# In the routing of a mixture of experts, TensorE's transposes of the next tile stand in front of the router's products of this one

## The chip, the cores and the metric

The program runs on one core of one Trainium2 chip. The metric is the device time of one execution in microseconds (us). TensorE multiplies and transposes, VectorE and ScalarE work on its results in the accumulation banks, GpSimd issues the gathers and scatters of rows, and SyncE issues the loads of the weights. Each engine runs its own instructions in the order in which they are written; between engines there are semaphores only.

## The reference, cut to what matters

Two blocks follow one another on 1024 tokens of width 1024. The second block has two layers, and each of them ends in the same mixture of experts, in which the experts choose their tokens:

```python
def expert_choice_moe(x, w_router, w_gate_up, w_down):
    B, S, _ = x.shape
    cap = CAPACITY_FACTOR * S // N_EXPERTS          # 128 tokens an expert
    aff = jax.nn.softmax((x @ w_router).astype(jnp.float32), axis=-1)
    gates, idx = lax.top_k(jnp.swapaxes(aff, 1, 2), cap)
    xs = x[bi, idx]
    g, u = jnp.split(jnp.einsum('becd,edf->becf', xs, w_gate_up), 2, axis=-1)
    out = jnp.einsum('becf,efd->becd', jax.nn.silu(g) * u, w_down) * gates[..., None]
    return jnp.zeros_like(x).at[bi, idx].add(out)
```

The change touches only how `x @ w_router` and its softmax are ordered on TensorE. There are 16 experts.

## The kernel before, in words

`moe` (from line 4210) is called once a layer, so twice. Its routing goes over the 1024 tokens in NT = 8 tiles of 128, in a loop `for k in range(NT + 2)` that stands once for each engine. Three sets of buffers are used in turn, `u = k % 3`: the banks 2u and 2u+1 belong to a set. For one tile the work is this chain:

1. T, TensorE, L4417: eight transposes of the tile of X into banks 2u and 2u+1. From tile 3 on, the first of them waits until VectorE has taken the affinities of the tile three back out of the same bank (`aff_taken`).
2. Copies, ScalarE, L4613: two copies, four blocks each, out of the two banks (even, odd) into a row of work memory that the trace names first_block or m_spare.
3. Products, TensorE, L4410: 16 small products with the router's weights, in two halves. The first waits for the even copy, the second for the odd one. Four strips of 32 partitions of bank 2u each collect a part of the sum.
4. Raw copy, ScalarE, L4627: the bank into m_logits.
5. Fold, TensorE, L4424: two products that add the four strips and turn the result round; it waits for the raw copy (`taken`).
6. Softmax: maximum and its negative on VectorE (L4797, L4799), exponential on ScalarE (L4618), reciprocal and scaling on VectorE (L4801, L4803).
7. One iteration of the loop later: the spread (L4386) and the turned affinities (L4433) on TensorE, the row copy on ScalarE (L4623), the copy of the turned affinities on VectorE (L4807, which frees the bank for T), and on VectorE a number of counts (L4751) for the rank of every token with expert 0. The number of counts grows with the tile.

The orders are written out by hand. In iteration k TensorE does: products of tile k-1, T of tile k, fold of tile k-1, spread and turned affinities of tile k-2. ScalarE does: the two copies of tile k, the exponential of tile k-1, the row copy of tile k-2, and last the raw copy of tile k (which needs the products that TensorE has in its iteration k+1). VectorE does: maximum to scaling of tile k-1, then copy and counts of tile k-2. From k = 8 on there is no T, and TensorE runs filler products of no use (`keep`, L180) that keep it busy.

When the loop is over, VectorE finishes the counts, ranks the tokens (L4774) and marks the chosen ones (L4780), TensorE multiplies them out to a list (`list_tensor`, L4392), runs 48 filler products, and waits for the list and for the rows that GpSimd gathers by it (L5025). These are transposed (L4447) and copied (L4643), and the products of expert 0 begin (L4461). SyncE has loaded the weights of expert 0 since the start of the stage.

The functions in question are given here with their lines.

Of the kernel before, what the change touches and what calls it, by code (L numbers as in the profile page):

```python
# [13 lines left out]
P = 128  # L14

D = 1024
KD = D // P
# [6 lines left out]
NT = SEQ // P  # L24
# [4185 lines left out]
def moe(k, c, ps, io, layer, X, rows, out, sb):  # L4210
# [7 lines left out]
    with stage(k, sb) as st:  # L4218
# [18 lines left out]
        turned, even, odd, logits, maxed, exped, inverted, affed, aff_turned, aff_taken = (st.sem(n) for n in (  # L4237
            "turned", "even_copied", "odd_copied", "logits", "maxed", "exped", "inverted", "affed", "aff_turned", "aff_taken"))
# [146 lines left out]
        def spread_tensor(pe, x, t):  # L4385
            pe.transpose(spread_bank(x, t), aff[:, t, x:x + 1].broadcast_to([P, P]), c["ident"][:, :]).then_inc(*spread[x].up())  # L4386
# [8 lines left out]
        def tensor(pe):  # L4395
            def keep(n):
                keep_streaming(pe, core, ps[5], n)

            pe.matmul(ps[7][:, 0:P], c["ones"][:, :], c["before"][:, :]).then_inc(*placed.up())
            for k in range(NT + 2):  # L4400
                if 1 <= k <= NT:
                    u = (k - 1) % 3
                    if k == 1:
                        pe.wait_ge(*router_in)
                    pe.wait_ge(even.sem, k)
                    for d in range(KD):
                        if d == 4:
                            pe.wait_ge(odd.sem, k)
                        q = slice(QUARTER * (d % 4), QUARTER * (d % 4) + QUARTER)
                        m = pe.matmul(ps[2 * u][q, 0:P], wr[:, d, :], spare[u][:, d, :], start=d < 4, stop=d >= 4)  # L4410
                    m.then_inc(*logits.up())
                if k < NT:
                    u = k % 3
                    if k >= 3:
                        pe.wait_ge(aff_taken.sem, k - 2)
                    for b in range(KD):
                        m = pe.transpose(ps[2 * u + b // 4][:, (b % 4) * P:(b % 4) * P + P], X[:, k, b * P:(b + 1) * P],  # L4417
                                         c["ident"][:, :])
                        if b % 4 == 3:
                            m.then_inc(*turned.up())  # L4420
                if 1 <= k <= NT:
                    u = (k - 1) % 3
                    pe.wait_ge(taken.sem, k)
                    pe.matmul(ps[2 * u + 1][:, 0:NE], raw[u][:, :], c["fold"][:, :]).then_inc(*brought.up())  # L4424
                if k >= 2:
                    u = (k - 2) % 3
                    pe.wait_ge(affed.sem, k - 1)
                    if k == 2:
                        pe.wait_ge(places_in.sem, 1)
                    elif k >= 4:  # L4430
                        pe.wait_ge(row_in.sem, k - 3)
                    spread_tensor(pe, 0, k - 2)
                    pe.transpose(ps[2 * u][0:NE, 0:P], aff[:, k - 2, 0:NE], c["ident"][:, :]).then_inc(*aff_turned.up())  # L4433
                if k >= NT:
                    keep(8)
# [647 lines left out]
        g, b = (spare[i][:, :, :].rearrange("p k t -> p (k t)") for i in range(2))  # L5083
# [20 lines left out]
        nc.gpsimd.memset(eps[:, :], LN_EPS).then_inc(*eps_set.up())  # L5104
        sync(nc.sync)
        tensor(nc.tensor)
        scalar(nc.scalar)
        vector(nc.vector)
# [96 lines left out]
```

## Time and profile before

| | |
|---|---|
| median of three runs | 3791.79 us (3790.16 to 3795.48) |
| the profiled execution's own time | 3789.95 us |
| its span | 3788.2 us |
| mean granted clock of TensorE | 0.994 |
| TensorE busy | 3679.2 us, 97% |
| VectorE busy | 2225.6 us, 59% |
| ScalarE busy | 1109.6 us, 29% |
| DMA, mean over the span | 152 GB/s |

The span runs from the first to the last instruction. A busy TensorE is not one at its peak: the filler counts as busy, and matmuls overlap. The routing of the first of the two layers lies at 1920 to 1966 us of the span, that of the second at 3069 to 3113 us.

### The profile page before, as it was taken

Reading aid. Unit: us, or ns where it says so; the run is one execution under the profiler, and the core shown is the slowest. Engines: PE = TensorE matmul, PEld = TensorE weight load, DVE = VectorE, ACT = ScalarE, POOL = GpSimd, SP = SyncE. Lnnn points to the kernel's source line nnn. Section 1 sums busy time; section 2 is a strip of 40 time slices with the busy share of each in tenths; the row PEclk is TensorE's granted clock in tenths of the full one; section 3 lists DMA queues with packets and bytes.
Section 4 is the critical chain, followed back from the end, with each engine's and each line's share of the span. In section 5 each row is a group of like instructions: output and inputs, shape, how many; then the busy total and the mean of one; then the engine's idle time right before and its main releaser. Section 6 shows DMA issues by size and latency. Waiting matters only on the chain. (4 is left out here: it accounts for less than half of the span.)

```text
span 3788.2 us, 63983 instructions
## 1 busy us (share of the span) xinstructions
PE 3679.2 (97%) x26734; PEld 1976.0 (52%) x26734; DVE 2225.6 (59%) x3869; ACT 1109.6 (29%) x2363; POOL 572.3 (15%) x709
## 2 busy tenths in 40 slices
PE   8999999999999999999999999998999999999998
PEld 5565756767586745545554433434444454343333
DVE  2234334666666645356667656664577788665664
ACT  2343313344353401046630111113343431111113
POOL 3332002011010022100001111110132201111110
PEclk9999999999999999999999999999999999999999
DMA  5101111000101052210069999996211259999996
GB/s 115 29 29 42 29 29 47 18 13 20 29 4 46 5 184 62 45 34 18 17 236 338 349 333 345 348 327 243 63 45 38 96 212 347 341 348 335 346 337 226
DMA packets 267326, 574.31 MB, mean 152 GB/s; under 512 B 49264, under 2 KB 123920, under 8 KB 267040
## 3 DMA queue, kind: packets, MB, share of 16 engines
q1 hardware_dynamic: 251776, 520.93, 38.9%
q0 software_dynamic: 9504, 34.61, 4.0%
q10 hardware_dynamic: 5760, 14.68, 1.0%
q8 instruction: 213, 3.49, 0.4%
q14 instruction: 73, 0.60, 0.0%
HBM read 521.93 MB, written 48.23 MB: 151 GB/s over the span
## 5 line engine op out<-in xcount | busy, mean ns | idle before, releaser
L4461 PE MATMUL bank<-ring,m_hidden_T 128*128 128x512 f32 x1024 | 449.4, 595 | 1.5 <-ACT m_hidden_T L4661 1.5
L4461 PEld LDWEIGHTS bank<-ring,m_hidden_T 128*128 128x128 f32 x1024 | 191.3, 190 | 232.6 <-issue 228.2
L4475 PE MATMUL bank<-ring,m_chosen 128*64 128x512 f32 x832 | 192.1, 604 | 4.0 <-POOL m_chosen L5041 4.0
L4475 PE MATMUL bank<-X,m_chosen 128*64 128x512 f32 x832 | 187.3, 592 | 0.0
L4881 DVE TENSOR_TENSOR m_junk<-bank,m_junk 128x512 f32<-128x512 f32 x26 | 18.0, 692 | 267.8 <-PE bank L4475 267.8
L4461 PE MATMUL bank<-ring,m_picked_T 128*128 128x512 f32 x384 | 167.9, 593 | 4.4 <-ACT m_picked_T L4643 2.4
L1683 PE MATMUL bank<-hnT,first_block 128*128 128x320 f32 (+3 forms) x512 | 167.7, 478 | 0.7 <-PEq L104 0.7
L4656 ACT ACTIVATE m_hidden<-m_junk 128x512 f32<-128x512 f32 x26 | 16.4, 632 | 447.6 <-DVE m_junk L4895 447.6
L4475 PEld LDWEIGHTS bank<-ring,m_chosen 128*64 128x64 f32 x832 | 58.2, 138 | 130.3 <-issue 124.6
L1683 PEld LDWEIGHTS bank<-hnT,first_block 128*128 128x128 f32 x512 | 94.5, 190 | 54.4 <-issue 11.7
L4858 DVE TENSOR_TENSOR X<-ring 128x1024 f32<-128x1024 f32 x104 | 122.5, 1221 | 0.0
L4868 DVE TENSOR_TENSOR X<-X,ring 128x1024 f32<-128x1024 f32 x104 | 122.2, 1217 | 0.0
L4475 PEld LDWEIGHTS bank<-X,m_chosen 128*64 128x64 f32 x832 | 59.8, 137 | 118.9 <-issue 118.9
L3401 PE MATMUL bank<-a_weights,xT 128*128 128x512 f32 x256 | 119.3, 594 | 1.3 <-DMA a_weights<-in_attn_w_o 1.3
L4461 PEld LDWEIGHTS bank<-ring,m_picked_T 128*128 128x128 f32 x384 | 72.0, 190 | 92.6 <-issue 89.8
L5070 POOL DMA_INDIRECT y_rows<-m_ys,m_tokens x30 | 47.7, 1590 | 480.4 <-issue 394.7
L1859 PE MATMUL bank<-rw_lane 64*64 64x64 f32 x2720 | 111.7, 224 | 8.7 <-issue 2.2
L532 PE MATMUL bank<-hnT,w_block 128*128 128x512 f32 (+3 forms) x304 | 119.4, 534 | 0.0
L4713 ACT ACTIVATE m_ys<-bank,m_gates 128x512 f32<-128x512 f32 x30 | 20.6, 687 | 328.9 <-PE bank L4461 328.9
L5025 POOL DMA_INDIRECT m_picked<-mix,m_tokens x32 | 53.5, 1673 | 408.1 <-PE bank L4447 217.8
L532 PE MATMUL bank<-hnT,first_block 128*128 128x512 f32 (+3 forms) x320 | 112.0, 501 | 0.6 <-PEq L104 0.6
L1859 PEld LDWEIGHTS bank<-rw_lane 64*64 64x64 f32 x2720 | 95.9, 133 | 28.9 <-issue 22.0
(683 smaller groups left out, 7691.9 us busy)
## 6 DMA issues: line engine op xcount, KB each, us to landing
ring<-in_moe_w_gate_up SPq DMA_DIRECT2D x90, 2048.0 KB, 9.6
ring<-in_moe_w_down SPq DMA_DIRECT2D x256, 512.0 KB, 4.9
ring<-in_moe_w_gate_up SPq DMA_DIRECT2D x96, 512.0 KB, 9.6
m_second_ring<-in_moe_w_gate_up SPq DMA_DIRECT2D x14, 2048.0 KB, 13.6
first_block<-in_w_in SPq DMA_DIRECT2D x23, 512.0 KB, 3.9
w_block<-in_w_in SPq DMA_DIRECT2D x19, 512.0 KB, 4.2
mix<-X SPq DMA_DIRECT2D x16, 512.0 KB, 2.6
ring<-y_rows SPq DMA_DIRECT2D x16, 512.0 KB, 8.4
```

The source lines that it names most:

```text
L532: x = pe.matmul(bank_of(s + j)[:, 0:w], wb[b % RING][:, d, :], hnT[:, d, col:col + w], start=d == 0, stop=d == KD - 1)
L1683: m = pe.matmul(banks[j][:, 0:n], wb[i % 3][:, d, :], hnT[:, d, col:col + n], start=d == 0, stop=d == KD - 1)
L1859: x = pe.matmul(L.tall(0)[side(d), h, i, :], power_t(L, e, d, h, i), power(L, e, d, h, i))
L3401: x = pe.matmul(ps[6 + half][:, :], oT[:, b, t * P:(t + 1) * P], weights[:, b, 512 * half:512 * half + 512], start=b == 0, stop=b == KD - 1)
L4461: m = pe.matmul(banks[j][:, :], lhsT[:, (i % 8) * P:(i % 8 + 1) * P], ring[:, i, j, :], start=i % 8 == 0, stop=i % 8 == KD - 1)
L4475: m = pe.matmul(bank[tok[half], :], tokens_(j), weights(j)[:, 512 * half:512 * half + 512], start=j == 0, stop=j == 3)
L4713: ac.activation(ys[:, 0:512], ps[6][:, :], ACT.Copy, scale=gates[:, e:e + 1]).then_inc(*y_even.up())
L4858: ve.tensor_tensor(t2(j), quarter(e, 2, j), quarter(e, 1, j), ALU.subtract).then_inc(*w_summed.up())
L4868: ve.tensor_tensor(t2(j), t2(j), quarter(e, 3, j), ALU.subtract).then_inc(*w_summed.up())
L4881: ve.tensor_tensor(u2[:, :], ps[1][:, :], first_kept[:, :], ALU.add).then_inc(*joined.up())
L5025: gp.indirect_dma_start(xg[:, :], None, rows_saved[:, :], bass.IndirectOffsetOnAxis(ap=tokens[:, e:e + 1], axis=0)).then_inc(*gathered.up(16))
L5070: gp.indirect_dma_start(y_rows[:, :], bass.IndirectOffsetOnAxis(ap=tokens[:, e:e + 1], axis=0), ys[:, :], None, compute_op=ALU.add).then_i ...
```

## The change

In TensorE's program the eight transposes of tile k are put in front of the products of tile k-1. Iteration k is now: T of tile k, products of tile k-1, fold of tile k-1, spread and turned affinities of tile k-2. The waits move along with their instructions. No instruction is added or taken away, and nothing is changed in the programs of the other engines.

```diff
             for k in range(NT + 2):
+                if k < NT:
+                    u = k % 3
+                    if k >= 3:
+                        pe.wait_ge(aff_taken.sem, k - 2)
+                    for b in range(KD):
+                        m = pe.transpose(ps[2 * u + b // 4][:, (b % 4) * P:(b % 4) * P + P], X[:, k, b * P:(b + 1) * P],
+                                         c["ident"][:, :])
+                        if b % 4 == 3:
+                            m.then_inc(*turned.up())
                 if 1 <= k <= NT:
                     u = (k - 1) % 3
                     if k == 1:
                         pe.wait_ge(*router_in)
                     pe.wait_ge(even.sem, k)
                     ...
                     m.then_inc(*logits.up())
-                if k < NT:
-                    u = k % 3
-                    if k >= 3:
-                        pe.wait_ge(aff_taken.sem, k - 2)
-                    for b in range(KD):
-                        m = pe.transpose(ps[2 * u + b // 4][:, (b % 4) * P:(b % 4) * P + P], X[:, k, b * P:(b + 1) * P],
-                                         c["ident"][:, :])
-                        if b % 4 == 3:
-                            m.then_inc(*turned.up())
                 if 1 <= k <= NT:
                     u = (k - 1) % 3
                     pe.wait_ge(taken.sem, k)
                     pe.matmul(ps[2 * u + 1][:, 0:NE], raw[u][:, :], c["fold"][:, :]).then_inc(*brought.up())
```

## Rows read from the trace of the kernel before

**Rows 1.** Chain that ended last, second layer: start us, us, what.
```profile
3079.85 1.09 ACT first_block L4613 x2
3084.66 1.90 DVE m_junk L4751 x12
3104.29 6.74 PE bank L180 x48
3111.03 0.89 PE bank L4447 x8
```

**Rows 2.** Timeline, TensorE, second layer: start, us, engine, line, operation [idle before].
```profile
3071.51 1.09 PE L4417 MATMUL bank<-ident,X 128*128 128x128 f32 x8
...
3076.43 1.09 PE L4417 MATMUL bank<-ident,X 128*128 128x128 f32 x8 [0.48 <-DVE m_aff L4807]
3077.36 0.29 PE L4424 MATMUL bank<-fold,m_logits 128*128 128x16 f32 x2
...
3077.84 0.84 PE L4410 MATMUL bank<-first_block,router 128*32 128x128 f32 x16
3079.16 1.09 PE L4417 MATMUL bank<-ident,X 128*128 128x128 f32 x8 [0.48 <-DVE m_aff L4807]
...
3087.94 1.09 PE L4417 MATMUL bank<-ident,X 128*128 128x128 f32 x8 [0.96 <-DVE m_aff L4807]
...
3090.59 0.40 PE L4424 MATMUL bank<-fold,m_logits 128*128 128x16 f32 x2 [0.40 <-ACT m_logits L4627]
```

**Rows 3.** Timeline, TensorE's weight loads for the second half of one tile's products, second layer.
```profile
3078.26 0.16 PEld L4410 LDWEIGHTS bank<-first_block,router 128*32 128x32 f32 x8 [0.26 <-ACT first_block L4613]
```

**Rows 4.** Timeline, VectorE, second layer.
```profile
3077.68 0.17 DVE L4797 TENSOR_REDUCE m_st<-bank 128x1 f32<-128x16 f32 x1 [0.77 <-PE bank L4424]
3077.89 0.15 DVE L4799 TENSOR_SCALAR m_st<-m_st 128x1 f32<-128x1 f32 x1
3078.49 0.16 DVE L4801 RECIPROCAL m_st<-m_st 128x1 f32<-128x1 f32 x1 [0.45 <-ACT m_aff_tiles L4618]
3078.69 0.23 DVE L4803 TENSOR_SCALAR m_aff_tiles<-m_aff_tiles,m_st 128x16 f32<-128x16 f32 x1
3078.83 0.27 DVE L4807 COPY m_aff<-bank 16x128 f32<-16x128 f32 x1
...
3090.35 0.27 DVE L4807 COPY m_aff<-bank 16x128 f32<-16x128 f32 x1
```

**Rows 5.** Timeline, ScalarE, second layer.
```profile
3077.12 1.09 ACT L4613 ACTIVATE first_block<-bank 128x512 f32<-128x512 f32 x2 [0.82 <-PE bank L4417]
3078.09 0.28 ACT L4618 ACTIVATE m_aff_tiles<-bank,m_st 128x16 f32<-128x16 f32 x1
...
3078.75 0.28 ACT L4627 ACTIVATE m_logits<-bank 128x128 f32<-128x128 f32 x1
...
3090.26 0.28 ACT L4627 ACTIVATE m_logits<-bank 128x128 f32<-128x128 f32 x1
```

**Rows 6.** DMA issues, 3104 to 3113 us: KB each (none for indirect ones), median us to landing.
```profile
m_picked<-mix,m_tokens POOLq DMA_INDIRECT x1, 4.4
```

**Rows 7.** Windows of 1 us, TensorE, first layer: length, busy (instructions), granted clock, DMA share, GB/s.
```profile
1923.00:1924.00 1.00, 1.00 (x14) 0.50 1.23 215
```

**Rows 8.** Windows, second layer: length, then busy (instructions) of TensorE, its loads, VectorE, ScalarE, GpSimd; clock.
```profile
3104.00:3106.00 2.00, 2.00 (x11) 2.00 (x11) 1.67 (x9) 0.00 (x0) 0.65 (x1) 0.50 0.19 76
```

**Rows 9.** Timeline, TensorE, first layer.
```profile
1923.52 1.97 PE L4417 MATMUL bank<-ident,X 128*128 128x128 f32 x8
1929.28 1.09 PE L4417 MATMUL bank<-ident,X 128*128 128x128 f32 x8 [0.48 <-DVE m_aff L4807]
1940.78 1.09 PE L4417 MATMUL bank<-ident,X 128*128 128x128 f32 x8 [0.96 <-DVE m_aff L4807]
```

**Rows 10.** Timeline, TensorE and GpSimd, around the list of expert 0, second layer.
```profile
3101.99 2.30 PE L4392 MATMUL bank<-m_aff_tiles,m_chosen 128*128 128x17 f32 x16 [1.21 <-DVE m_chosen L4780]
3105.35 0.98 POOL L5025 DMA_INDIRECT m_picked<-mix,m_tokens  x1 [35.98 <-DVE m_gates L4785]
```

## The prediction

> **What bounds the kernel now.** I read the page's first two parts, then the chain of waits, then the timeline of the routing engine by engine. The chain runs almost wholly over TensorE's expert products, but in both layers it also runs through the routing, end to end: VectorE's counts, ScalarE's copies, the filler, the transposes of the gathered rows [rows 1]. So a microsecond in the routing is a microsecond of the kernel, unless something near its end gives it back. Time was lost in the routing although no engine is full: T of tile 3 starts at 3076.43, T of tile 4 at 3079.16, and ahead of each TensorE sits idle 0.48 us for VectorE's copy [rows 2]. The routing is a ring of waits over three engines.
>
> The ring before, tile 3 to tile 4, start to start: T to fold 0.93 (3076.43 to 3077.36) [rows 2]; fold to maximum 0.32, to the negative 0.21 [rows 4]; to the exponential 0.20 (3078.09) [rows 5]; to the reciprocal 0.40, to the scaling 0.20, to the copy 0.14 [rows 4]; to the next T 0.33 (3079.16) [rows 2]. Sum 2.73 us. The products are not in this ring: they run at 3077.84 to 3078.68, behind the fold and ahead of the next T, while VectorE and ScalarE work on the softmax, and the raw copy (3078.75) [rows 5] is done long before the next fold asks for it. They look slow, 0.84 us with a wait of 0.26 us for the odd copy in the middle [rows 2, 3], but it lies beside the softmax and costs nothing.
>
> **The change part by part.** Nothing is added; two pieces change places on TensorE. T of tile k+1 still can't start before VectorE's copy. Behind it now come the products of tile k, whose operands were copied a tile ago, and only then the fold of tile k, which needs the raw copy of those products. What lay beside the softmax is put into the ring.
>
> *The ring after.* T to the first product 0.93, as T to fold before. The products no longer wait. How long do sixteen take in one go? Eight take 0.42 from first start to last end (3078.26 to 3078.68), with weights loaded in 0.16 [rows 2, 3]; sixteen take 0.42 + 0.16 = 0.58 if the second eight follow at the pace of the loads. Below: all within 0.42. Above: 0.84, as with the waits. I take 0.58, since the loads' pace is the nearest row. Last end to raw copy 0.07 (3078.68 to 3078.75) [rows 2, 5]. So the raw copy starts at 0.93 + 0.58 + 0.07 = 1.58 after T. Raw copy to fold 0.33 (3090.26 to 3090.59, the one case where TensorE waited for it) [rows 5, 2]: 1.91. To the exponential by VectorE 0.32 + 0.21 + 0.20: 2.64. But there is a second rule: ScalarE does the raw copy of tile k before the two copies of tile k+1, and before the exponential. In front of it the copies start 0.69 after T (3077.12) and the exponential stands 0.97 behind their start [rows 5]. Now they start only behind the raw copy, at 1.58 + 0.16 (its 0.28 less the overlap of some 0.12 that the two copies show, 1.09 us for a pair of which the second ends 0.12 after the next start) = 1.74, and the exponential can start at 2.71. This is later than 2.64, so it decides. Then 0.40 + 0.20 + 0.14 + 0.33 as before: 3.78 us. The ring grows by 1.05.
>
> The Trainium skill, "TensorE: Matmul & The Clock Gate", section "Part 3: Packing small matmuls — row/col tiling", has it that products that write different strips of 32 partitions run at once, three of them 2.38 times as fast as one by one. The rows agree with it as far as they go, since the loads of eight products are through in 0.16 us and the last ends 0.26 us later. By that rule the sixteen would lie nearer the lower bound, 0.42, and the ring would be 3.62.
>
> *VectorE's counts* stood in the ring for the late tiles: T of tile 7 waits 0.96 [rows 2]. From copy to the next possible maximum there are now 0.33 + 1.91 + 0.32 = 2.56 us, of which the counts can use 2.36 (they start 0.20 behind the copy), and for tile 3 they last 1.90 [rows 1], so they go under: T of tile 3 to T of tile 7 took 11.51 (3076.43 to 3087.94; first layer 1929.28 to 1940.78, 11.50) [rows 2, 9] and will take 4 x 3.78 = 15.12. That is +3.61 a layer. Behind T of tile 7 the order on TensorE is the old one, and VectorE full of counts is the bound. Its copy came 2.41 after T (3090.35) [rows 4] and now comes at 2.71 + 0.74 = 3.45: +1.04. All counts, the list and the gather shift with it.
>
> *The first tiles* gain. T of tile 1 starts right behind T of tile 0, at 3070.32 in place of 3071.51 [rows 2]. By the same steps the raw copy of tile 0 comes at 3071.9 and T of tile 2 at 3072.4; products of tile 1 start behind it (3073.33) and T of tile 3 at 3076.2: -0.2. In the first layer the clock is at half there (0.50 in 1923 to 1924, T of tile 1 1.97 us long) [rows 7, 9]; T and the products now both stand ahead of the first fold in this stretch, and the gain is eaten: 0.
>
> Sum so far: first layer 3.61 + 1.04 = 4.65, second 4.45; together +9.1.
>
> *The end of the routing.* GpSimd issues the gather at 3105.35 and it has landed 4.4 later, 3109.75 [rows 6, 10], but the transposes of its rows start only at about 3110.9, behind the filler [rows 1]. Of a delay there up to 1.1 us a layer could come back, if the filler runs at full clock (a part of it ran at half [rows 8]). Where the low stretch falls after a shift of over 4 us I can't tell: -0.1 on the whole, with ends 0 and -2.2. Weights of expert 0 have landed before the list in both cases, so they hide nothing; the expert stage behind starts as it did, only later.
>
> Forecast: +9.0. On the profiled execution, 3789.95, that is 3799.0. The median of the runs shown is 1.84 higher, 3791.79, so the median after should be 3800.8.
>
> **The rivals.**
>
> (a) *The clock falls inside the ring.* TensorE now works about 2.1 us of 3.78 a tile, with an idle stretch of some 1.3 us where 0.48 stood. Against a fall: idle 0.96 before T of tile 7 did not bring it down. For: in both layers it fell after the idle 1.21 before the list [rows 10, 8] (and in the first before 1923 [rows 7]). At the lower of its levels (1.2 GHz in place of 2.4) T lasts 1.97 in place of 1.09 [rows 9], +0.88, and the products and the fold lose another 0.4. At 1.3 us a tile and two to five such tiles a layer this is +5 to +13 on top, about 3808. The skill's same page, "A second HAM failure mode: psum-queue depth-cycling", tells of small pauses between groups of matmuls that make the clock go down and up; no row of this ring shows it so far.
>
> (b) *Muted.* Products at 0.42 (-0.16 in each of 5 rings and twice in the first tiles, -1.1 a layer) and the filler's slack used in full (-1.1 a layer): 9.1 - 4.4 = 4.7, time 3796.5. For it speaks that strips overlap, against it that both must be at their end.
>
> (c) *Faster.* T ahead of the products starts the two copies earlier, and the products find their operands ready. If the copy to T wait were not what holds T, the 1.2 us by which T of tile 1 is early would be kept in each layer, and the idle 0.48 ahead of T would go in five tiles a layer: -2.4 to -7.2, 3784.6 to 3789.4. It decides if fold does not have to wait for the raw copy. The rows speak against it: the idle ahead of T names the VectorE copy, which stands behind the fold, and the raw copy can't precede its products.
>
> **How the numbers follow.** Forecast 0.52 (its own range 3799.0 to 3804.5: products between the pace of the loads and 0.84, +0.26 in 12 rings at most), (a) 0.25, (b) 0.19, (c) 0.04. The range goes from 3796 to 3811. What can be told from no change is about 0.2%, 7.6 us, which is 3799.4. Forecast and (a) lie above it but for a small part of the forecast's case: slower 0.76, same 0.20, faster 0.04.
>
> **What would show it.** Start to start of T in tiles 3 to 7 at 3.78, not 2.73; idle ahead of T for VectorE's copy grown to 1.3 or so; a new idle stretch of TensorE of 0.4 ahead of every fold, released by the raw copy; the copies (L4613) directly behind the raw copy; no wait left ahead of the products. TensorE's granted clock below 1 between T of tile 3 and T of tile 7 would be (a). If T follows T by under 3.4 us, or the list comes less than 3.5 us later behind the stage's start, the sum is wrong; if T follows T by 2.73 or less, the reasoning is.

## The result: 14 us slower, a ratio of 1.0042

The changed kernel takes 3805.05 us (median of six runs, 3803.64 to 3811.04) against 3790.97 us (six runs, 3786.28 to 3795.48): ratio 1.0042, 95% interval 1.0032 to 1.0051. The profiled execution took 3805.19 us with a span of 3803.4 us; before 3789.95 and 3788.2. The forecast was slower by 9.0 us, 3800.8, with a range of 3796 to 3811. Direction, mechanism and range held; the slowdown was 5 us more than forecast.

T of tile 0 of the first layer stands at 1924.39 in place of 1921.13, with the same instructions ahead of it. Two kernels with nearly the time of before have it at 1924.5 and 1924.6 (first_tiles and b_bank2, below; b_bank2 has the old order), so these 3.3 us aren't tied to the change. Everything below is measured from T of tile 0 in each layer.

The counts of TensorE's matmuls in all texts here are those of the trace. It lists each f32 product of the program as two instructions and each transpose as one: the fold is one `pe.matmul` and stands as x2, the products of a tile are eight and stand as x16, `keep(24)` stands as x48.

The routing after, TensorE, second layer, one tile and the end of the ring (start, us, engine, line, operation [idle before]); T is now L4406, the products L4419:

```profile
3093.09 1.09 PE L4406 MATMUL bank<-ident,X 128*128 128x128 f32 x8 [1.24 <-DVE m_aff L4807]
3094.11 0.64 PE L4419 MATMUL bank<-first_block,router 128*32 128x128 f32 x16
3095.16 0.40 PE L4424 MATMUL bank<-fold,m_logits 128*128 128x16 f32 x2 [0.40 <-ACT m_logits L4627]
...
3097.05 1.09 PE L4406 MATMUL bank<-ident,X 128*128 128x128 f32 x8 [1.24 <-DVE m_aff L4807]
...
3101.01 1.09 PE L4406 MATMUL bank<-ident,X 128*128 128x128 f32 x8 [1.24 <-DVE m_aff L4807]
3102.04 1.08 PE L4419 MATMUL bank<-first_block,router 128*32 128x128 f32 x16
3103.52 0.61 PE L4424 MATMUL bank<-fold,m_logits 128*128 128x16 f32 x2 [0.40 <-ACT m_logits L4627]
...
3106.95 3.62 PE L180 MATMUL bank<-ones 128*128 128x128 f32 x16
```

Before, T followed T at 2.73 us with 0.48 idle ahead of it [rows 2]. Now it is 3.96 us, 1.24 idle ahead of T, and 0.40 idle ahead of the fold, released by the raw copy (m_logits). The products have no wait any more. Behind T of tile 7, at 3101.01, the same products take 1.08 in place of 0.64 us and sixteen filler matmuls 3.62 us: the clock has fallen, as the windows below show. ScalarE's timeline in the same tile:

```profile
3094.82 0.28 ACT L4627 ACTIVATE m_logits<-bank 128x128 f32<-128x128 f32 x1 [2.27 <-PE bank L4419]
3095.00 1.08 ACT L4613 ACTIVATE m_spare<-bank 128x512 f32<-128x512 f32 x2
3095.99 0.27 ACT L4618 ACTIVATE m_aff_tiles<-bank,m_st 128x16 f32<-128x16 f32 x1
```

VectorE's timeline in the same tile:

```profile
3095.59 0.17 DVE L4797 TENSOR_REDUCE m_st<-bank 128x1 f32<-128x16 f32 x1 [1.05 <-PE bank L4424]
3095.80 0.15 DVE L4799 TENSOR_SCALAR m_st<-m_st 128x1 f32<-128x1 f32 x1
3096.38 0.16 DVE L4801 RECIPROCAL m_st<-m_st 128x1 f32<-128x1 f32 x1 [0.43 <-ACT m_aff_tiles L4618]
...
3096.72 0.27 DVE L4807 COPY m_aff<-bank 16x128 f32<-16x128 f32 x1
```

The copies come directly behind the raw copy, as foretold, where they stood 0.69 behind T [rows 5]. The chain of waits of the changed kernel (start, us, what), same layer, behind the ring:

```profile
3117.91 1.71 PE bank L4392 x16
...
3119.87 14.57 DVE m_junk L4751 x72
...
3151.93 0.70 DVE m_hidden L4919
3152.67 0.66 PE bank L4454 x4
```

Here the chain leaves the list (L4392) over VectorE: the 36 counts for expert 1 (72 instructions, a count and the reading of its sum), its ranking, the first rounds of the selection for the other experts, and only then the hidden values of expert 0. In the kernel before it went over the filler, the gathered rows and expert 0 [rows 1]. The two ways are nearly equally long: the transposes of those hidden values (L4454) start 34.9 to 35.0 us behind the list after, and 35.3 to 35.4 before. This matters below.

The windows of TensorE in the changed kernel, second layer (length, busy, instructions, granted clock, DMA share, GB/s):

```profile
3099.00:3102.00 3.00, 1.64 (x12) 1.00 1.04 384
3102.00:3105.00 3.00, 2.60 (x31) 0.51 1.04 410
...
3108.00:3111.00 3.00, 3.00 (x16) 0.50 1.03 410
```

The times in the routing, from T of tile 0 of each layer, in us ("3 to 7" is T of tile 3 to T of tile 7; each from TensorE's timeline):

| kernel | T of tile 3 | 3 to 7 | list | first product of expert 0 |
|---|---|---|---|---|
| before, layer 1 | 8.15 | 11.50 | 33.71 | 44.84 |
| before, layer 2 | 7.05 | 11.51 | 32.61 | 43.75 |
| after, layer 1 | 7.07 | 15.84 | 39.65 | 49.52 |
| after, layer 2 | 7.06 | 15.84 | 39.64 | 49.35 |

The list comes 5.94 and 7.03 us later, together 12.97. Of these, 8.67 come from tile 3 to 7, 5.37 from behind T of tile 7, and 1.07 are gained ahead of tile 3.

### The profile page after: what moved, and what is told of

It is laid out like the page before. It is cut to its first block and busy times, and to the rows that moved or that the text cites. A ratio compares the mean times of both kernels' runs of the same rounds, so it can differ in the third digit from the quotient of the medians.

```text
span 3803.4 us, 63983 instructions
## 1 busy us (share of the span) xinstructions
PE 3684.1 (97%) x26734; PEld 1980.8 (52%) x26734; DVE 2226.9 (59%) x3869; ACT 1107.4 (29%) x2363; POOL 570.2 (15%) x709
## 5 line engine op out<-in xcount | busy, mean ns | idle before, releaser
L4475 PE MATMUL bank<-ring,m_chosen 128*64 128x512 f32 x832 | 192.1, 604 | 4.0 <-POOL m_chosen L5041 4.0
L4475 PE MATMUL bank<-X,m_chosen 128*64 128x512 f32 x832 | 187.3, 592 | 0.0
L4475 PEld LDWEIGHTS bank<-ring,m_chosen 128*64 128x64 f32 x832 | 58.2, 138 | 130.5 <-issue 124.7
L4475 PEld LDWEIGHTS bank<-X,m_chosen 128*64 128x64 f32 x832 | 59.7, 137 | 118.8 <-issue 118.8
```

The lines of the kernel that those rows point to most:

```text
L4475: m = pe.matmul(bank[tok[half], :], tokens_(j), weights(j)[:, 512 * half:512 * half + 512], start=j == 0, stop=j == 3)
```

## The experiments

Medians in this section are those of the runs of one chip, each with the ratio to the kernel before on that chip (3790.08, 3789.84 and 3790.05 us in the three sets). List times are from T of tile 0, first and second layer.

**The changed kernel once more** (a_again, no edit).

> The changed kernel once more. Theory: the change costs what the routing shows, so the ring (T of tile 3 to T of tile 7) is 15.8 us in both layers against 11.5, T of tile 0 to the first product of expert 0 about 49.4 us, and the total 10 to 13 us over the kernel before. T of tile 0 of the first layer, which stood 3.3 us later in the changed kernel's trace, isn't tied to the change: it can stand anywhere from 1919 to 1926. Rival: the 3.3 us ahead of the routing belong to the change as well and stand there again (1924 or later), total 14 us or more.

3809.26 us, ratio 1.0054 (1.0040 to 1.0067). In its trace tile 3 to 7 is 16.69 and 15.84, first product at 50.29 and 49.39, T of tile 0 at 1924.00. The trace agrees with the theory within a few tenths but for one tile. The median, 19 us over the kernel before, is above the 10 to 13 expected. In the first layer something was left out of the theory:

```profile
1942.95 1.28 PE L4406 MATMUL bank<-ident,X 128*128 128x128 f32 x8 [1.24 <-DVE m_aff L4807]
1944.16 1.08 PE L4419 MATMUL bank<-m_spare,router 128*32 128x128 f32 x16
...
1947.76 1.97 PE L4406 MATMUL bank<-ident,X 128*128 128x128 f32 x8 [1.00 <-DVE m_aff L4807]
```

T to T is 4.81 us here: the clock fell inside the ring (0.50 from 1946 to 1949 us). This costs 0.85 us, and the profiled execution took 3804.21 us, the fastest of the five, so this trace alone doesn't show where the 19 us come from. The runs' mean granted clocks point at more such falls: of the eleven runs of this kernel five have 0.993 or 0.994 and 3803.6 to 3805.2 us; the six with 0.990 to 0.992 have 3808.1 to 3814.4 us. None of the six was traced. T of tile 0 stands at 1924.00, just at the rival's mark, but the rival, that the 3.3 us ahead of the routing belong to the change, falls with b_bank2, which has the old order and 1924.56.

**The idle ahead of T filled** (a_keep2, against the changed kernel).

```diff
                     pe.transpose(ps[2 * u][0:NE, 0:P], aff[:, k - 2, 0:NE], c["ident"][:, :]).then_inc(*aff_turned.up())
+                if 2 <= k < NT - 1:
+                    keep_streaming(pe, core, ps[2 * ((k - 2) % 3) + 1], 4)
```

> The changed kernel with eight filler matmuls in the idle stretch of 1.24 us ahead of T in tiles 3 to 7. Theory: the ring is waits, not TensorE's work, so it stays 15.8 us from T of tile 3 to T of tile 7 although TensorE does 0.94 us more a tile; the granted clock stays at 1.00 behind T of tile 7, and T of tile 7 to the list falls from 16.7 to about 15.3 us. Total 1 to 3 us under the changed kernel. Rival, TensorE's own work bounds the ring: it grows by up to 0.9 us a tile. Rival, the low clock behind T of tile 7 costs nothing: T of tile 7 to the list stays 16.7.

3799.21 us, ratio 1.0025 (1.0015 to 1.0035), with runs of 3798.0 to 3803.0. Tile 3 to 7 stays 15.85 and 15.84, and T of tile 7 to the list is 15.30 in place of 16.74 in both layers, with the clock at 1.00 in both. TensorE's timeline in one tile of the second layer:

```profile
3090.54 0.64 PE L4419 MATMUL bank<-first_block,router 128*32 128x128 f32 x16
3091.58 0.40 PE L4424 MATMUL bank<-fold,m_logits 128*128 128x16 f32 x2 [0.40 <-ACT m_logits L4629]
...
3092.07 1.06 PE L180 MATMUL bank<-ones 128*128 128x128 f32 x8
3093.48 1.09 PE L4406 MATMUL bank<-ident,X 128*128 128x128 f32 x8 [0.35 <-DVE m_aff L4809]
```

And TensorE's windows behind T of tile 7 of the first layer, columns as above:

```profile
1949.00:1952.00 3.00, 2.60 (x33) 1.00 1.02 407
1952.00:1955.00 3.00, 2.45 (x22) 1.00 1.02 406
```

More work on TensorE made the kernel faster. The ring is not TensorE's work, and the low clock is part of what the change costs. The gain against the changed kernel is 6 to 10 us by the medians, over the 1 to 3 expected. The list accounts for 2.9 of it; the rest would be falls inside the ring in runs that weren't traced, which the expectation left out, but that is not shown. What is left over the kernel before, 9.1 us, is the ring at full clock; the list is later by 4.50 and 5.60 us there, 10.1.

**The move for tiles 0 to 2 alone** (first_tiles, here against the kernel before).

```diff
+                if k < 3:
+                    ...
                 if 1 <= k <= NT:
                     ...
-                if k < NT:
+                if 3 <= k < NT:
```

> The move done for tiles 0 to 2 alone, from tile 3 on the old order. Theory: the loss is in the tiles whose T waits for VectorE's copy. T of tile 3 to T of tile 7 is 11.5 us as before, T of tile 0 to T of tile 3 about 7.1 (before 8.15 and 7.05), total within 2 us of the kernel before. Rival, a T ahead of the products costs something in every tile: T of tile 0 to T of tile 3 grows by about 1 us a tile.

3790.88 us, ratio 1.0002 (0.9993 to 1.0011). T of tile 3 at 7.06 and 7.07, tile 3 to 7 11.51 and 11.50, list 32.63 in both layers. As the theory has it: all the loss is in the tiles whose T waits for VectorE's copy.

**ScalarE's order turned round** (a_scalar_order): the raw copy of tile k-1 behind the copies of tile k, in the changed kernel.

```diff
                     for half, done in enumerate((even, odd)):
                         ...
+                if 1 <= k <= NT:
+                    ac.wait_ge(logits.sem, k)
+                    ac.activation(raw[(k - 1) % 3][:, :], ps[2 * ((k - 1) % 3)][:, 0:P], ACT.Copy).then_inc(*taken.up())
                 ...
-                if k < NT:
-                    u = k % 3
-                    ac.wait_ge(logits.sem, k + 1)
-                    ac.activation(raw[u][:, :], ps[2 * u][:, 0:P], ACT.Copy).then_inc(*taken.up())
```

> The changed kernel, but on ScalarE the raw copy of a tile stands behind the two copies of the next one, no longer ahead of them. Theory (two rules for the exponential, ScalarE's queue deciding by 0.1 us): the copies start 0.7 us behind T, the raw copy stays at 1.73, the exponential comes at 2.79 by VectorE in place of 2.89, and the ring is 3.86 us in place of 3.96. Rival (ScalarE's order alone makes the loss): the ring falls to 3 us or less.

One run, 3805.77 us. The ring is 3.96 us at full clock (second layer), not 3.86: a miss. The raw copy comes at 1.73 and the exponential at 2.89, as without the edit, but now VectorE releases it. TensorE's timeline:

```profile
3090.32 1.09 PE L4406 MATMUL bank<-ident,X 128*128 128x128 f32 x8 [1.24 <-DVE m_aff L4806]
3091.34 0.64 PE L4419 MATMUL bank<-first_block,router 128*32 128x128 f32 x16
3092.38 0.40 PE L4424 MATMUL bank<-fold,m_logits 128*128 128x16 f32 x2 [0.40 <-ACT m_logits L4617]
```

ScalarE's:

```profile
3092.05 0.28 ACT L4617 ACTIVATE m_logits<-bank 128x128 f32<-128x128 f32 x1
3093.21 0.27 ACT L4621 ACTIVATE m_aff_tiles<-bank,m_st 128x16 f32<-128x16 f32 x1 [0.88 <-DVE m_st L4798]
```

VectorE's:

```profile
3092.81 0.17 DVE L4796 TENSOR_REDUCE m_st<-bank 128x1 f32<-128x16 f32 x1 [1.46 <-PE bank L4424]
```

From the fold to the maximum it is 0.43 us, not 0.32: a fold that had to wait takes 0.40, one that follows directly 0.29. By VectorE the exponential is thus also due at 2.89. The two rules meet within a hundredth, and ScalarE's order costs nothing in the ring. Ahead of it T of tile 3 came at 7.29 in place of 7.06 in both layers. And the clock fell inside the ring in both: tile 3 to 7 is 19.79 us in the first layer and 16.59 in the second. The first layer:

```profile
1935.57 1.97 PE L4406 MATMUL bank<-ident,X 128*128 128x128 f32 x8 [0.99 <-DVE m_aff L4806]
...
1940.85 1.09 PE L4406 MATMUL bank<-ident,X 128*128 128x128 f32 x8 [1.25 <-DVE m_aff L4806]
...
1945.38 1.97 PE L4406 MATMUL bank<-ident,X 128*128 128x128 f32 x8 [0.99 <-DVE m_aff L4806]
```

With that, three of the six layers traced with the new order and no filler in it (after, a_again, this one) have a fall inside the ring.

**A bank of its own for the turned affinities** (b_bank2 with the old order, a_bank2 with the new one). T then waits for the exponential of the tile three back.

```diff
                     if k >= 3:
-                        pe.wait_ge(aff_taken.sem, k - 2)
+                        pe.wait_ge(exped.sem, k - 2)
                     ...
+                    if k >= 3:
+                        pe.wait_ge(aff_taken.sem, k - 2)
-                    pe.transpose(ps[2 * u][0:NE, 0:P], aff[:, k - 2, 0:NE], c["ident"][:, :]).then_inc(*aff_turned.up())
+                    pe.transpose(ps[7][0:NE, 0:P], aff[:, k - 2, 0:NE], c["ident"][:, :]).then_inc(*aff_turned.up())
```

VectorE's copy reads bank 7 accordingly. The spread is kept in bank 6 alone and waits for the row copy of the tile before.

> The kernel before, with the turned affinities in a bank of their own (bank 7; the spread then has bank 6 alone), so that T waits for the exponential of the tile three back and no longer for VectorE's copy. Theory: the ring over VectorE's copy is open. T follows T at 2.0 to 2.5 us in tiles 3 and 4 and then runs ahead of VectorE, whose own work (1.35 us plus the counts, 2.4 to 3.2 us a tile) is left as the bound. T of tile 0 to the list falls by 1 to 2 us a layer. Rival (T's place in the order is what counts): no change.

> The changed kernel with the same bank of its own for the turned affinities. Theory: the change costs only because T waits for VectorE's copy and the products and the raw copy then stand behind T in that ring; with the ring open it costs nothing. T of tile 0 to the list within 1.5 us of the kernel before with the same bank, total within 3 us of it, so 10 us or more under the changed kernel. Rival, the fold waits for the raw copy in any case: T of tile 0 to the list stays 3 us or more above the kernel before with that bank.

Old order 3787.74 us, ratio 0.9991 (0.9982 to 1.0000); new order 3788.45 us, 0.9994 (0.9985 to 1.0003). T follows T at 2.19 us with the old order and 2.50 with the new; the list stands at 31.55 and 31.56 against 31.97 and 31.97. TensorE's timeline with the new order, second layer:

```profile
3077.14 1.04 PE L4406 MATMUL bank<-ident,X 128*128 128x128 f32 x8
3078.11 0.64 PE L4419 MATMUL bank<-first_block,router 128*32 128x128 f32 x16
3079.15 0.40 PE L4424 MATMUL bank<-fold,m_logits 128*128 128x16 f32 x2 [0.40 <-ACT m_logits L4629]
...
3079.64 1.04 PE L4406 MATMUL bank<-ident,X 128*128 128x128 f32 x8
```

The 0.40 us ahead of the fold are still there, the 1.24 ahead of T are gone. The move by itself costs 0.4 us a layer up to the list, and the two times can't be told apart; all the rest of its price needs the wait for VectorE's copy.

**The products done twice** (b_twice, a_twice): the loop over d stands over `[*range(KD), *range(KD)]`.

> The kernel before with each tile's sixteen router products done twice over. Theory: the products lie beside the softmax and outside the ring, with 0.48 us of idle behind them, so 0.3 us more a tile cost nothing up to tile 7: T of tile 3 to T of tile 7 stays 11.5 us. Rival (TensorE's work is the bound): it grows by 0.3 us a tile.

> The changed kernel with each tile's sixteen router products done twice over. Theory: here the products are in the ring, so each tile grows by what the second sixteen add, 0.3 to 0.4 us: T of tile 3 to T of tile 7 goes from 15.84 to 17.0 to 17.5 us, the total up by 4 to 6 us. Rival (products outside of the ring here too): stays 15.8.

Old order 3791.56 us, ratio 1.0004 (0.9994 to 1.0013), tile 3 to 7 11.50 and 11.50: nothing in the ring. Ahead of it they do cost: T of tile 3 is at 7.93 in place of 7.05, and the list at 33.50 in place of 32.61 (second layer). TensorE's timeline in the second layer:

```profile
3079.15 1.28 PE L4410 MATMUL bank<-first_block,router 128*32 128x128 f32 x32
3080.47 1.09 PE L4417 MATMUL bank<-ident,X 128*128 128x128 f32 x8
...
3083.21 1.09 PE L4417 MATMUL bank<-ident,X 128*128 128x128 f32 x8
```

T still follows T at 2.74 us: the products fill the idle time that stood ahead of it.

New order 3816.77 us, ratio 1.0069 (1.0054 to 1.0085). At full clock its ring is 4.40 us (first layer, tile 3 to 4), +0.44, what the second sixteen take (1.08 less 0.64). Tile 3 to 7 came out at 22.9 and 21.1 us, over the 17.5 expected, and the total 8 to 12 us over the changed kernel, not 4 to 6, since the clock falls again and again. The windows of TensorE in the second layer:

```profile
3091.00:3095.00 4.00, 2.64 (x45) 1.00 1.03 387
...
3099.00:3103.00 4.00, 3.01 (x23) 0.50 1.05 376
3103.00:3107.00 4.00, 2.36 (x38) 0.93 1.05 391
3107.00:3111.00 4.00, 3.35 (x40) 0.60 1.06 390
```

The same instructions are free inside the old ring and paid in the new one, 0.44 us a tile at full clock: this shows most directly what came into the ring.

**Eight more filler matmuls ahead of the list** (b_keep: kernel before; b_bank_keep: with the bank of its own, old order): `keep(16)` becomes `keep(20)` ahead of `list_tensor(pe, 0, ps[4])`.

> The kernel before with eight more filler matmuls in the idle stretch of 1.2 us ahead of the list of expert 0. Theory: that stretch makes the clock fall, and the 48 filler matmuls behind the list then run for about 7.1 us in place of 5.6, with the gathered rows waiting behind them. With the stretch filled, list to transposes of the gathered rows falls from 8.87 to about 7.6 us (the gather, landed 7.6 us behind the list's start, is then the bound), the total by up to 2.6 us. Rival (the clock falls at that place anyhow): 8.87 stays.

> The old order with the turned affinities in a bank of their own, and the same eight filler matmuls more ahead of the list. Theory: both effects add up, list to transposes 7.6 us, T of tile 0 to the list 31.6 us, total 3 to 5 us under the kernel before. Rival: as with the bank alone, 2 us under it.

The mechanism came as expected. TensorE's timeline in b_keep:

```profile
3101.47 1.96 PE L4392 MATMUL bank<-m_aff_tiles,m_chosen 128*128 128x17 f32 x16 [0.33 <-DVE m_chosen L4780]
3103.28 5.60 PE L180 MATMUL bank<-ones 128*128 128x128 f32 x48
3108.91 1.07 PE L4447 MATMUL bank<-ident,m_picked 128*128 128x128 f32 x8
```

List to the transposes of the gathered rows fell from 8.87 and 8.88 to 7.69 and 7.44 us, and expert 0 began 1.2 and 1.4 us earlier behind the list. The gain did not come: b_keep 3791.20 us, ratio 1.0000 (0.9991 to 1.0009). b_bank_keep has 3786.32 us, ratio 0.9990 (0.9981 to 0.9999), which can't be told from b_bank2. Its list stands at 32.61 and 31.55 us, not 31.6 in both: in the first layer the clock fell behind T of tile 7 (0.50 from 1946 to 1949 us), with the old order, so a fall there doesn't need the change. The chain of waits of b_keep goes the way of the changed kernel's:

```profile
3103.69 14.57 DVE m_junk L4751 x72
...
3135.75 0.70 DVE m_hidden L4919
3136.49 0.66 PE bank L4454 x4
```

From the list to the first product of expert 2 (L4475) it is 100.5 to 101.0 us in both layers of all twelve traces, whether expert 0 begins 9.7 or 11.2 us behind the list. The list sets the time; what the filler and the gather take is covered by VectorE but for these tenths.

## Why the prediction was right, and where its sum was short

*The ring.* Right in kind: the products and the raw copy came into the ring, T still waited for VectorE's copy, and the idle moved to where it was looked for. 3.96 us measured, 3.78 forecast, by three small terms. T to the first product is 1.02, not 0.93 as to the fold; the products take 0.64, not 0.58; fold to maximum is 0.43 behind a wait, not 0.32. The first two bring the raw copy to 1.73 in place of 1.58. That ScalarE's queue alone decides was wrong: with the third term VectorE is as late (a_scalar_order). The forecast's way over VectorE, 3.71 in all, comes to 3.97 with the three terms. Four rings: 4.34 and 4.33 a layer, forecast 3.61.

*VectorE's counts* go under the longer ring as forecast: every ring is 3.96, and the wait of 0.96 ahead of tile 7 [rows 2] is now 1.24 like all others.

*The first tiles.* Forecast 0 and -0.2, measured -1.08 and +0.01. In the first layer the kernel before had lost 1.1 us there to the low clock [rows 9]; in the changed kernel's trace the clock stayed up. b_keep, with the order of before in these tiles, has T of tile 3 at 7.05 too: that is chance and not the change, and it hid 1.1 us of the shortfall.

*Behind T of tile 7*: forecast 1.04, measured 2.68 and 2.69. This is the term that was mis-sized. 1.24 of it is the ring's own growth. The other 1.44 is the low clock: in a_keep2, with the clock up, the stretch is 15.30 in place of 16.74, and in the first layer of a_scalar_order, where the clock was up again behind T of tile 7 and nothing was filled, it is 15.28. It acts by longer products and folds, by filler that runs 3.62 us for sixteen ahead of the turned affinities, and by filler still running when the list could start.

*The end of the routing.* Forecast -0.1 with ends 0 and -2.2, on the ground that a shorter filler would give back part of the delay. The filler did run at full clock (5.60 us behind the list), and expert 0 began 1.3 and 1.4 us earlier behind the list, but that is worth only 0.2 and 0.5 us (list to expert 2, 100.8 and 101.0 before, 100.6 and 100.5 after): VectorE's chain is nearly as long (b_keep). So of the 12.97 us some 12.3 count. The medians differ by 14.1; where the other 2 us lie isn't shown, since the slower runs have no trace. My statement that the expert stage starts as it did, only later, overlooked a second chain next to the critical one.

*Rivals.* (a), the clock falls inside the ring, had 0.25 and came in part. Not in the profiled execution, where it fell right behind T of tile 7, but in one layer of a_again and in both of a_scalar_order. The runs of the changed kernel with the lower mean clock, six of eleven, lie 3 to 11 us above the others; that their falls were inside the ring is likely, not shown. (a) was priced at +5 to +13 on top, up to 3813.8, which is outside the stated range. Leaving the low clock out of the likeliest case is the larger part of what made the sum short: 2.9 of the 3.9 us by which the list is later than forecast. All six layers traced with the new order and no filler have a fall in the ring or behind it. (b) is refuted: sixteen products took 0.64 and not 0.42, and the slack behind the list is worth 0.7 us in all and not 2.2. (c) is refuted by the 0.40 ahead of every fold; the 1.2 us by which T of tile 1 is early was lost again by tile 3 (7.06 against 7.05).

One figure of the forecast doesn't follow from its own text: the upper end 3804.5 of its own range needs 14 rings of +0.26, as (b) counts them, and not the 12 that it names.

The Trainium skill, "TensorE: Matmul & The Clock Gate", section "Part 3: Packing small matmuls — row/col tiling", says that products on different strips run at once; the estimate from it was a ring of 3.62. The trace agrees that they overlap: sixteen more products add 0.44 us (a_twice), 0.03 each, against 0.12 for each full-width transpose (0.93 for eight). But sixteen took 0.64 and not the lower bound of 0.42, and the ring 3.96. On the same page the Trainium skill's section "A second HAM failure mode: psum-queue depth-cycling" tells of small pauses that make the clock go down and up. The trace of a_twice agrees: 1.00, 0.50, 0.93, 0.60 in the windows above, with pauses of 1.24 and 0.40 us in a tile at full clock.

Left open: how often the clock falls in each place, and why it fell in one tile and not in the next of the same length. Only the profiled executions show where; of the other runs there is only the mean.

## What to carry to other kernels

Before an instruction is moved ahead on an in-order engine, go round the ring of waits and ask whether what it passes was beside the ring or in it: the products were free where they filled the wait for another engine; behind that wait they cost their full length plus the copy that follows them. Where a buffer's release closes the ring, look first at who holds it last; a bank of its own brought the two orders to within 0.4 us a layer. A stage's delay is to be followed over all chains that leave it, not only the one printed as critical, and idle added to TensorE in every step is to be priced with its clock.

## What the runs showed of the hardware

- Products on strips of 32 partitions behind full-width transposes start 1.02 us after the first of the eight; a full-width fold in the same place started at 0.93. (In a_bank2, where T didn't wait, they start at 0.97.) Their weight loads had 0.17 us of idle ahead of them, put down to issue.
- A fold behind a wait of 0.40 us takes 0.40 us, one right behind transposes 0.29, both at a granted clock of 1.00. The maximum behind it starts 0.43 and 0.32 us after the fold.
- Filler matmuls in an idle stretch of 1.24 us a tile (0.35 left) kept the granted clock at 1.00 in and behind the ring in the trace of a_keep2, and the median was 6 to 10 us lower; without them it stood at 0.50 from 3102 to 3111 us.
- No single idle stretch in the ring was over 1.25 us where the clock fell inside it (a_again, a_scalar_order), and 1.24 and 0.40 us of idle in every 3.96 us also went by for several tiles at 1.00.
